# A state-space scan rewritten from a loop of eight serial turns into one unrolled block

## The reference, cut to what matters

```python
def mamba2_branch(z, xbc, dt_raw, conv_w, conv_b, dt_bias, a_log, d_skip, norm_g):
    xbc = silu(causal_conv(xbc, conv_w, conv_b))          # 4 taps, 1024 channels
    xs, bm, cm = split(xbc, [512, 512 + 256])             # x, B, C
    dt = softplus(dt_raw + dt_bias); a = -exp(a_log)
    y = ssd_chunked(xs, dt, a, bm, cm) + xs * d_skip
    y = y * silu(z)                                       # gate
    y = rms_norm_2(y, norm_g)                             # over each group of 256 channels

def ssd_chunked(xs, dt, a, bm, cm):                       # per chunk c of 128 tokens, per head
    a_cum = cumsum(dt * a)                                # within the chunk
    seg = exp(where(tril, a_cum[l] - a_cum[s], -inf))     # 128 x 128 decay matrix
    y_diag = ((cm @ bm.T) * seg) @ (xs * dt)
    states = bm.T @ (xs * dt * exp(a_cum[-1] - a_cum))
    y_off = (cm * exp(a_cum)) @ state                     # state before the chunk
    state = state * exp(a_cum[-1]) + states               # the only recurrence
```

## Time and profile before

| | |
|---|---|
| median of 3 runs | 5148.59 us (5147.55 to 5153.25) |
| profiled execution: its time | 5148.16 us |
| profiled execution: its span | 5146.3 us |
| busy share of the span: PE, PEld | 81%, 58% |
| busy share: DVE, ACT, POOL | 42%, 29%, 17% |
| mean granted TensorE clock | 0.883 of full |

### The profile page before, as it was taken

The page is one execution under the profiler, slowest core; times in us unless marked ns, Lnnn a source line. Parts: engine busy times, 40 slices in busy tenths (PEclk is TensorE's granted clock), DMA queues, the critical chain, the costliest instruction groups (busy, mean ns, idle before and its releaser), DMA issues. The chain is left out here.

```text
span 5146.3 us, 45404 instructions
## 1 busy us (share of the span) xinstructions
PE 4150.6 (81%) x17034; PEld 2982.0 (58%) x17034; DVE 2160.6 (42%) x2568; ACT 1483.9 (29%) x2331; POOL 890.4 (17%) x386
## 2 busy tenths in 40 slices
PE   6698699978696899777667888874699875799996
PEld 6576455557574455555446555553477764566663
DVE  0293366632463676322374111315212202566665
ACT  1211245531112445210313333312210101455551
POOL 0142300002343000023110111120234322100001
PEclk6799799989898899888888998986799985899997
DMA  4111112222111021123221101220233230799995
GB/s 147 57 37 31 31 65 83 74 84 96 33 43 39 25 68 55 62 78 37 38 49 45 13 12 12 23 26 0 25 43 49 31 131 35 280 379 380 379 346 217
DMA packets 351721, 470.70 MB, mean 91 GB/s; under 512 B 46301, under 2 KB 217282, under 8 KB 351042
## 3 DMA queue, kind: packets, MB, share of 16 engines
q1 hardware_dynamic: 338770, 423.88, 28.4%
q0 software_dynamic: 7888, 26.78, 1.4%
q10 hardware_dynamic: 4896, 17.83, 0.9%
HBM read 396.59 MB, written 71.86 MB: 91 GB/s over the span
## 5 line engine op out<-in xcount | busy, mean ns | idle before, releaser
L1089 PE MATMUL values<-probs,vp 128*128 128x512 f32 x672 | 348.9, 601 | 12.0 <-issue 6.4
L1178 ACT ACTIVATE probs<-scores 128x512 f32<-128x512 f32 (+1 forms) x336 | 196.1, 584 | 309.2 <-PE scores L211 307.5
L1387 POOL TENSOR_TENSOR out_hi<-out_w,ones 128x1024 fp32r<-128x1024 f32 x24 | 57.3, 2388 | 1197.6 <-DMA out_w<-in_w_out 1197.6
L209 PE MATMUL scores<-q_hi,k_rest 97*128 97x512 f32 (+1 forms) x336 | 262.4, 781 | 0.0
L676 DVE SCALAR_TENSOR_TENSOR conv_out<-conv_in,vectors,conv_out 128x1295 f32<-128x1295 f32 (+1 forms) x120 | 254.3, 2119 | 4.3
L2927 PE MATMUL dp<-h_t,abt 128*128 128x512 f32 x544 | 241.9, 597 | 1.9 <-ACT abt L2975 1.9
L209 PE MATMUL gates_ps<-x_t_r,gates_w_r 128*128 128x512 f32 (+1 forms) x560 | 210.3, 376 | 22.0 <-POOL gates_w_r L257 22.0
L209 PE MATMUL out_ps<-h_t_r,out_w_r 128*128 128x512 f32 (+1 forms) x448 | 172.2, 384 | 67.8 <-POOL out_w_r L1389 67.8
L2957 ACT ACTIVATE expert_hi<-wu 128x1024 fp32r<-128x1024 f32 x136 | 144.9, 1065 | 253.2 <-PE gp L211 253.2
L1260 DVE TENSOR_REDUCE mx<-made 128x1 f32<-128x640 f32 (+1 forms) x272 | 203.6, 793 | 27.1 <-PE made L1030 26.5
L210 PE MATMUL gates_ps<-h_t_r,gates_hi 128*128 128x512 f32 (+1 forms) x560 | 209.9, 375 | 0.0
(11 more groups left out here) (517 smaller groups left out, 10247.6 us busy)
## 6 DMA issues: line engine op xcount, KB each, us to landing
wg<-in_w_gate SPq DMA_DIRECT2D x34, 2048.0 KB, 10.1
wu<-in_w_up SPq DMA_DIRECT2D x34, 2048.0 KB, 11.7
h_t<-in_w_down SPq DMA_DIRECT2D x34, 2048.0 KB, 10.1
slot_rows<-zero_rows SPq DMA_DIRECT2D x16, 1536.0 KB, 9.7
ahead_w<-in_w_ada SPq DMA_DIRECT2D x48, 512.0 KB, 3.8
slot_rows<-yb ACTq DMA_DIRECT2D x34, 512.0 KB, 8.1
gates_w<-in_w_in SPq DMA_DIRECT2D x28, 512.0 KB, 3.9
mod_w<-in_w_mod SPq DMA_DIRECT2D x12, 1024.0 KB, 5.1
```

What stands on the lines that cost most here:

```text
L209: nc.tensor.matmul(out, lhs[1], rhs[0], start=start, stop=False, **kw)
L1089: nc.tensor.matmul(O[b % 2][:, 0:w], vp[g // 2 % 2][:, kb, g % 2 * VD:g % 2 * VD + P], pr[m % 3][:, 0:w], start=kb == 0, stop=kb == nk - 1 ...
L1178: nc.scalar.activation(pr[m % 3][:, 0:w], S[m % 2][:, 0:w], ACT.Exp, scale=scale).then_inc(s.exped, 1)
```

## The change

It concerns `state_space` and one new argument of `conv_gemm`.

- Stage 2 is left out (`activated=True`). Silu over `xbc` is instead issued by ACT ahead of its evacuations of the two gate pairs (`activate(0, 3)`: six tiles, `activate(3, 4)`: two tiles).
- Stage 3 is left out. Its DMAs are issued by SP in the new block; the first chunk starts the state, so that nothing is cleared.
- The loop over chunks becomes one block with one barrier, unrolled for 8 chunks. Each engine has its own order of work, in which the parts of chunk c + 1 that don't need the state stand ahead of the part of chunk c that does.
- POOL takes over `ua` (`spread`), the product ea·C (`decay_c`, now in place) and the gating (`gated`).
- The subtraction of the column sums goes into the bias of the exp, which becomes 8 ACT instructions for each chunk, one for each head, with a [128, 1] bias from `nacol`. The mask is added by PE: two fp32r products of an identity with the mask, accumulated onto `rows`.
- The copies `xc`, `adt`, `dtc` and `acol` go; all column sums come from one product ahead of the loop. `dec` (8 numbers a head row) is made by a small exp for each chunk.
- `xdt`, `xdec`, the state, `bt`, `ea`, `seg` and the PSUM tile for B and C·B have two buffers; `ua`, `rows`, the transposed x, `yt`, y's and the state's PSUM tiles have one. `ea` and `seg` lie in the context columns of `k.h` and `k.x`.
- Stage 5 is left out; its four norms are in the same block, the first two within chunks 4 to 7, the last two behind the last chunk.

The core of the diff:

```diff
-def conv_gemm(nc, k, name, w_in, first, convs, wt, bias, more):
+def conv_gemm(nc, k, name, w_in, first, convs, wt, bias, more, activated=False):
...
         split_gemm(nc, k, name, parts, X_BLOCKS, extra=("conv_steps", convolve))
+    if activated:
+        return
...
+        def activate(first, last):
+            def before(act, s, g):
+                act.wait_ge(s.conv_steps, 2 * TAPS * (2 + last))
+                for c in range(2 * first, 2 * last):
+                    nc.scalar.activation(xbc[:, c, :], xbc[:, c, :], ACT.Silu)
+            return before
...
-        with nc.Fori(0, NT2) as c, stage(nc, names) as s, nc.Block() as block, ExitStack() as es:
+        with stage(nc, names) as s, nc.Block() as block, ExitStack() as es2:
...
             @block.gpsimd
+                spread(0)
+                spread(1)
+                decay_c(0)
+                for c in range(NC):
+                    if c + 2 < NC:
+                        spread(c + 2)
+                    if c + 1 < NC:
+                        decay_c(c + 1)
+                        pool.wait_ge(s.yt_made, 4 * (c + 1))
+                        y = k.y[:, 0:4, here(c)]
+                        nc.gpsimd.tensor_tensor(y, y, yt[:, :, :], ALU.mult).then_inc(s.gated, 1)
...
             @block.tensor
+                def prepare(c):
+                    pe.wait_ge(s.ua_made, c + 1)
+                    if c:
+                        pe.wait_ge(s.seg_made, c)
+                    for i in range(2):
+                        m = nc.tensor.matmul(rows[:, 4 * i:4 * i + 4, :], k.ones[:, :], ua[:, 4 * i:4 * i + 4, :],
+                                             start=True, stop=True, skip_group_check=True)
+                    m.then_inc(s.rows_made, 1)
...
+                    pe.wait_ge(s.ea_made, 2 * (c + 1))
+                    for i in range(2):
+                        m = nc.tensor.matmul(rows[:, 4 * i:4 * i + 4, :], ident_r[:, :], over_heads(after_r[:, :], 4),
+                                             start=False, stop=True, skip_group_check=True)
+                    m.then_inc(s.masked, 1)
...
+                prepare(0)
+                for c in range(NC):
+                    if c + 1 < NC:
+                        prepare(c + 1)
...
+                    if c in (5, 6):
+                        add_norm(c - 5)
+                    pe.wait_ge(s.mt_made, 2 * (c + 1))
+                    if c:
+                        pe.wait_ge(s.cd_made, 2 * (c + 1))
+                        pe.wait_ge(s.st_made, c)
+                        pe.wait_ge(s.yt_made, 4 * c)
+                    for h in range(H):
...
+                add_norm(2)
+                add_norm(3)
...
             @block.scalar
+                def weights(c):
+                    act.wait_ge(s.rows_made, c + 1)
...
+                    act.wait_ge(s.masked, c + 1)
+                    for h in range(H):
+                        m = nc.scalar.activation(seg[c % 2][:, h, :], rows[:, h, :], ACT.Exp, bias=nacol[:, c, h:h + 1])
+                    m.then_inc(s.seg_made, 1)
...
+                weights(0)
+                for c in range(NC):
+                    if c + 1 < NC:
+                        weights(c + 1)
+                    if c in (4, 5):
+                        square(c - 4)
+                    if c in (5, 6):
+                        root(c - 5)
+                square(2)
+                square(3)
+                root(2)
+                root(3)
...
             @block.vector
+                dve.wait_ge(s.d_in, 32)
+                spread_x(0)
+                weigh(0)
+                for c in range(NC):
+                    if c + 1 < NC:
+                        spread_x(c + 1)
+                        carry(c)
+                        weigh(c + 1)
+                    add_skip(c)
+                    if c >= 6:
+                        norm(c - 6)
+                dve.wait_ge(s.yt_made, 4 * NC)
+                y = k.y[:, 0:4, here(NC - 1)]
+                nc.vector.tensor_tensor(y, y, yt[:, :, :], ALU.mult).then_inc(s.gated_last, 1)
+                norm(2)
+                norm(3)
```

More of the change, by code:

```diff
@@ L2361, in state_space @@
[L2361 to L2370, removed]
@@ L2371, in state_space, with spread @@
-        with nc.Fori(0, NT2) as c, stage(nc, names) as s, nc.Block() as block, ExitStack() as es:
[L2372 to L2379, removed]
+                def spread(c):
+                    if c:
+                        pool.wait_ge(s.rows_made, c)
+                    nc.gpsimd.tensor_tensor(ua[:, :, :], over_heads(k.mats[:, UPTO, :], H),
+                                            over_tokens(k.decay[:, c, 0:H], H, P), ALU.mult).then_inc(s.ua_made, 1)
@@ L2388, in _ @@
[L2388 to L2394, removed]
+                nc.scalar.activation(nacol[:, :, :], s_ps[:, :, 0:NC], ACT.Copy, scale=-1.0).then_inc(s.col_kept, 1)
@@ new lines, in square @@
+                def square(i):
+                    half, g = norms[i]
+                    if half:
+                        act.wait_ge(s.gated, NC - 1)
+                        act.wait_ge(s.gated_last, 1)
+                    else:
+                        act.wait_ge(s.gated, NC // 2)
+                    if i >= 2:
+                        act.wait_ge(s.summed, i - 1)
+                    for c in range(2):
+                        nc.scalar.activation(sq[i % 2][:, c, :], normed_part(i, c), ACT.Square).then_inc(s.squared, 1)
@@ new lines, in root @@
+                def root(i):
+                    act.wait_ge(s.summed, i + 1)
+                    if i >= 2:
+                        act.wait_ge(s.normed, 2 * (i - 1))
+                    nc.scalar.activation(rt[i % 2][:, :], norm_ps[:, :], ACT.Ln, bias=k.eps, scale=1.0 / 256).then_inc(s.logged, 1)
+                    act.wait_ge(s.logged, i + 1)
+                    nc.scalar.activation(rt[i % 2][:, :], rt[i % 2][:, :], ACT.Exp, scale=-0.5).then_inc(s.rooted, 1)
+                weights(0)
@@ L2409, in _ @@
[L2409 to L2423, removed]
@@ new lines, in weigh @@
+                def weigh(c):
+                    dve.wait_ge(s.seg_made, c + 1)
+                    if c < NC - 1:
+                        dve.wait_ge(s.xdt_made, c + 1)
+                        if c >= 2:
+                            dve.wait_ge(s.s_made, c - 1)
+                        nc.vector.tensor_tensor(xdec[c % 2][:, :, :], xdt[c % 2][:, :, :],
+                                                seg[c % 2][:, :, P - 1:P].broadcast_to([P, H, HD]), ALU.mult).then_inc(s.xdec_made, 1)
+                        dve.wait_ge(s.xdec_made, c + 1)
+                    dve.wait_ge(s.pair_made, c + 1)
+                    for g in range(G):
+                        m = seg[c % 2][:, R * g:R * g + R, :]
+                        nc.vector.tensor_tensor(m, over_heads(bc_ps[c % 2][:, G + g, :], R), m, ALU.mult).then_inc(s.mt_made, 1)
@@ new lines, in add_skip, with norm @@
+                def add_skip(c):
+                    dve.wait_ge(s.y_made, c + 1)
+                    if c:
+                        dve.wait_ge(s.gated, c)
+                    for j in range(4):
+                        nc.vector.scalar_tensor_tensor(yt[:, j, :], xbc[:, j, here(c)], dcol[:, j:j + 1], y_ps[:, j, :],
+                                                       ALU.mult, ALU.add).then_inc(s.yt_made, 1)
+                def norm(i):
+                    half, g = norms[i]
+                    dve.wait_ge(s.rooted, i + 1)
+                    for c in range(2):
+                        y = normed_part(i, c)
+                        nc.vector.scalar_tensor_tensor(y, y, col(k, "ssm_norm", 2 * g + c), rt[i % 2][:, :], ALU.mult, ALU.mult)\
+                            .then_inc(s.normed, 1)
```

190 lines of the change are left out of this document (120 added, 70 removed).

## The result

The changed kernel takes 4982.03 us (median of four, 4978.69 to 4986.43) against 5149.0 us before: ratio 0.967, 95% interval [0.966, 0.969], so faster by 167 us. The forecast was 5021, faster by 128, with a range from 5006 to 5052.

What follows compares the result with a forecast made beforehand. No engine was taken to bound the old stretch; the new chunks were to be bound by a ring through all engines. Terms 12.1 + 9.0 + 27.6 + 16.0 + 3.85 + 13.5 = 82.0 us replace 209.3, giving 5020.9; range 5006 to 5052.

Steps and rivals of the forecast that it cites:

- The stretch: From conv_gemm's last evacuation to the last norm product: 82.0 us forecast in place of 209.3.
- start: Term 1, ahead of chunk 0: barrier, POOL's first ua, rows, transpositions, mask and seg, PE at the low clock, 12.1 us.
- chunks 1 to 4: Term 3, scan: 6.9 us for each chunk, set by the ring through all engines, 27.6 us in all.
- chunks 5 and 6 with the wait for y(7): Scan: 8.0 us each with four more PE norm-sum instructions, then 1.85 us until chunk 6's skip is done; 17.85 us.
- y(7) and what is behind it: End of the scan: y of chunk 7, then skip, gate and remaining norms; 15.5 us.
- the ring through all engines: Scan: dependency cycle over PE, ACT, DVE and POOL carrying two chunks, 13.7 us, or 6.85 for a chunk.
- what is taken out here goes from the total one for one: Whole kernel: the stretch lies between barriers with nothing in flight across, so its saving of 127.3 us is the total's.
- Other stages changed in length: Outside the stretch: listed as a sign that the prediction is wrong; no size or chance given.
- Low clock: Rival, scan: PE's clock stays low, its ring is 11.7 us, 37 us more, total 5058; chance 0.1.
- POOL the bound: Rival, scan: slower POOL tiles set the pace, 5 to 23 us more, total 5026 to 5044; chance 0.1 beyond 5033.
- No look-ahead in fact: Rival, scan: a single buffer ties each chunk to the one before, 12.0 us for a chunk, total 5057; chance 0.08.
- Silu 0, d_skip 0: Silu moved into conv_gemm and d_skip's load at the block's start are covered and cost 0 us; uncovered Silu 8 us.

Runs made afterwards that it cites:

- e6: Changed kernel, constant expert turn count, TensorE making prepare(c + 1) behind y(c) in place of ahead of it (no look-ahead): 5031.03 us.
- e7: Changed kernel, constant expert turn count, the norm back as a stage of its own behind the scan: 4986.06 us, ratio 0.9687.
- e11: Changed kernel, constant expert turn count, with an unused input of 2.1 MB ahead of all others: 4968.58 us.
- e4: Changed kernel, constant expert turn count, Silu over the convolved channels back in a stage of its own: 4996.41 us.
- e12: Changed kernel, constant expert turn count, with an unused input of 8.4 MB ahead of all others: 4979.46 us.
- e5: Changed kernel, constant expert turn count, with an unused input of 4.2 MB ahead of all others: 4965.46 us, ratio 0.9648.
- e1: Kernel before, with only the experts' turn count made a constant 1 in place of a loaded value: 5145.4 us, ratio 0.9991.
- e10: Kernel before, constant expert turn count, with an unused input of 8.4 MB ahead of all others: 5106.21 us, ratio 0.9916 to before.

## Why the prediction was wrong

*The stretch was right, 82.0 against 79.2.* By its terms: start 12.1, measured 9.0; chunk 0 9.0, measured 8.8; chunks 1 to 4 27.6, measured 26.8; chunks 5 and 6 with the wait for y(7), 17.85, measured 18.2; y(7) and what is behind it 15.5, measured 16.4. I had put the start 3 us too high for two reasons: POOL's first `ua` took 1.90 us, not 2.37, as nothing ran beside it, and PE was still at the full clock from `conv_gemm`, so `rows` took 1.82 and not 3.55 to the first transposition, and what follows it was quicker too. The second reason is luck: in e6, e7 and e11 the same start fell to the low clock, as I had assumed. In chunks 1 to 4 I had named the ring through all engines (6.85) as the longer; it is PE's own, 6.70, longer than my 6.3 because y's 32 instructions take 1.95 and not 1.76, and mask and state 0.57 and 0.96 and not 0.47 and 0.86; the mask's start, 3.23 behind `rows`, was right. PE was therefore busy 0.98 of the time and not 0.85.

*The step that failed is "what is taken out here goes from the total one for one".* It takes the rest of the kernel as given, since nothing is in flight across the borders and the code there is the same; what the change does outside its stretch was put at 0 us, and it was 33.7. The runs show that this rest isn't given: the same instructions took 4891 to 4936 us outside the scan in the kernel before, and 4885 to 4902 in the new one, by the size of an unused input, and up to 4910 in e4 and e6, where only the scan or the place of the Silu had changed. The step was sound as to the scan, which takes 130 us off in the trace. For the other 34 us the prediction had no mechanism. The kernel before reaches stages as short with 8.4 MB ahead of its inputs, so they don't need the new scan, but how much of them is placement, how much the clock's course in the weight stages, and whether the new code has a part, stays open. The range had no term for any of this, and 34 us on one side was more than its lower margin of 15. "Other stages changed in length" stood in the list of what would show the prediction wrong, without a chance or a price.

*Low clock (0.1).* It didn't come: 1.00 in chunks 1 to 6, and 0.79 only in y(7) and the norm behind it. Transpositions are six of a chunk's 52 PE instructions (208 in four chunks), and the window over chunks 1 to 4 is at 1.00. The Trainium skill's TensorE: Matmul & The Clock Gate, "PE-mode transpose", by which these don't count as busy in the same way, would speak against the change; in this trace the clock stayed up all the same. e6 shows the mechanism in part: a clock of 0.80 and 13.6 us for a chunk.

*POOL the bound (0.1).* No, but only just: its own work is 6.58 us for a turn of 6.70, where I had 6.0. Contention there was, but it fell on DVE as well, which I had put at 0.05 us: the kept state waits for 0.70 us, and `ua` takes 2.35 beside it and 1.90 alone. By the Trainium skill, SBUF — State Buffer, "SBUF: two separate sides", one of the two engines holds the shared ports for a whole instruction and the other waits; in the turn shown the kept state starts 0.44 us into POOL's gate and ends with 0.70 us more, and the `ua` behind it is 0.45 longer, so the trace agrees, and it shows that both pay in turn.

*No look-ahead in fact (0.08).* No: e6, where PE has none, is 49 us slower.

*Silu 0, d_skip 0.* Both right in the sum; e4 gives what the Silu costs without cover. For d_skip the reason was wrong: in the new kernel's trace DVE's first `xdt` waits for that DMA until 3440.36, over 2 us after the first transpositions of x were made, and ends at 3441.05. It is free because `seg`, which the next step needs as well, is ready at 3441.95 only.

What also stays open is what in a program's placement makes packets slow, and what changed it between the two kernels without a pad, whose inputs are the same. Nor is it explained why e12, with packets of 36.3 ns, has longer weight stages than e5. I didn't try to move single tensors. With a pad alone the new kernel comes to 4965.46 us (e5, ratio 0.9648 [0.9632, 0.9664]) and 4968.58 (e11, 0.9646), the fastest here, but that is luck of two sizes and no rule.

## What to carry to other kernels

A change to one stage of a large kernel may shift others whose code it doesn't touch: widen the range by some 20 to 40 us in 5000 where stages live from the landing of 512-byte packets, and take the change's own effect from the stage's borders in the trace, not from the total. A pad of unused memory, at several sizes and on both kernels, shows for one line of code how far the rest moves by itself; one size would have misled here. And where an overlap keeps TensorE without gaps, count it twice: once for the chain that it hides, once for the clock; a separate stage ahead of a burst of products costs its own length, and it can cost their first microseconds too.

## What I had not expected of the hardware

- The kernel before, with no instruction changed, took 5145.4 us without (e1) and 5106.2 with 8.4 MB of unused input ahead of its weights (e10); the mean packet of 512 bytes that carries `ssm_w` took 82.2 and 60.2 ns, while in the stretch of the first block's `gates_w` loads packets of that size took 31.7 and 31.6.
- A VectorE instruction on 128x512 with two SBUF inputs took 0.68 us alone and 1.38 in the median beside GpSimd; GpSimd's 128x1024 took 1.90 alone and 2.34 beside VectorE.
- TensorE's clock in the first chunk was 0.66 in one program and 1.00 in another with the same scan: 8.8 and 6.3 us for the same instructions.
